# Weighted expert sums as 64x64 quarters in four banks, and conditioning products in four column groups

## The chip, the cores and the metric

The kernel runs on one core of a Trainium2 chip. The core has five engines that run side by side: TensorE (matrix products, with its own loading of weights), VectorE, ScalarE, GpSimd (in the profile POOL; here it issues the gathers) and SyncE (which issues plain transfers). The metric is the device time of one execution in microseconds (us). The kernel before took 2040.57 us, the median of three runs (2038.49 to 2043.5).

## The reference, cut to what matters

One layer of a decoder for 512 prompt rows and 8 sample rows of 1024 values, all in fp32. Two parts of it matter here. The first is the conditioning: `m = silu(c) @ w_ada + b_ada`, with nine rows of `c` (one prompt, eight samples) and 6144 columns, split into the six shifts, scales and gates. The second is the retrieval of experts, after the attention and the pooling:

```python
def block(args):                       # 128 rows at a time
    hb, eb, gb = args                  # rows, 8 heads x 16 experts each, their gates
    act = gelu(einsum('td,thkd->thk', hb, u_tab[eb]))
    return einsum('thk,thkd->td', gb * act, v_tab[eb])
```

So each of 512 rows has 128 experts of its own. For each one a row of 1024 values of `u_tab` is gathered for a dot product, and a row of `v_tab` to be added up, weighted by the gate times the activation. That is 2 x 512 x 128 rows of 4 KB, 537 MB, in four blocks of 128 rows.

## The kernel before, in words

Everything lives in one tensor, `arena`, of 128 partitions, and in eight banks of PSUM, each 128 partitions by 512 columns. The order of each engine is written out by hand; semaphores tie the engines together. A plan (`bank_plan`) lists what uses a bank in which order; each takes the next bank in turn, and TensorE waits until ScalarE ("A") or VectorE ("V") has read the bank's former content (`begin`, `wait_emptied`).

**Conditioning.** `w_ada` comes in twelve blocks of 512 columns (2 MB each) through a ring of three places that all weights of the first part share. SyncE issues a block when the use of the place's former content has ended. `ada_products(i)` (L1119 to L1123) is eight products that add up in one bank: the stationary side is a 128x9 piece of the transposed conditioning, the moving side 128x512 weights. ScalarE copies the 9x512 result out (L513), and `ada(i)` turns it with four transposes (L1130). VectorE adds the bias. Blocks 0 to 3 come first of all, since the first normalisation needs them; 4 to 6 stand behind the attention, 7 behind the branch products, 8 to 11 before the second normalisation.

**Experts.** A block of 128 rows has 32 steps of four expert slots each, in eight turns of four steps. A step goes through the engines so:
- GpSimd issues four gathers of 128 rows of `u_tab` and four of `v_tab` (L464), each into 128 partitions, one row to a partition. There are two sets of buffers for each table; a gather waits until the step before last has used its set.
- VectorE forms the four dot products (L956), and later the coefficients (L961).
- ScalarE applies the gelu (L614) and then writes four diagonal matrices, 128x128, with the coefficients on the diagonal (L618).
- TensorE multiplies each diagonal with the gathered 128x1024 rows in two halves of 512 columns, and adds up in two PSUM banks (L1351, `expert_step`). Blocks alternate between banks 0, 1 and 2, 3; `clear_sums` (L1342) zeroes them first.
- At a block's end VectorE multiplies the two banks by the gate `g2b` (L1001), adds the residual rows, which TensorE has transposed into two more banks (L1395), and SyncE stores the rows. This is `finish(b)`; it stands behind turn 0 of the next block.

In turn 0 VectorE's dot products read the normalised rows from SBUF; from turn 1 on they read them from PSUM, into which TensorE transposes them (L1402) after turn 0.

The first 16 steps of block 0 are interleaved with the products by the query weights (`pq`, L1104, 16 pieces of 0.5 MB) and the scores of the experts' keys (L1335, L1337), which route the tokens. Routing of the next block runs in VectorE's steps of the block before. In block 3 the eight sample rows are prepared between the turns, in banks 0 and 1, and their own gathers and sums come last (L1428, L1439).

## Time and profile before

| | us |
|---|---|
| median of three runs | 2040.57 |
| the profiled execution | 2038.34 |
| its span, first to last instruction | 2036.3 |
| TensorE busy in the span | 1662.0 |
| VectorE busy | 1075.1 |
| GpSimd busy | 1042.4 |
| ScalarE busy | 367.2 |
| expert products (L1351), busy | 1002.7 |

The span of a profiled execution is cut into stretches, and for each the profile gives the busy time of the engines, the granted share of TensorE's clock (1.00 is 2.4 GHz, 0.50 is 1.2 GHz) and what the transfers moved. The chain of waits follows the work that ended last back from the end: at each step it goes to what released the wait, so that a piece in it is on the path. A row of TensorE's timeline merges equal instructions; a bracket behind it tells how long the engine sat idle before and what ended that. An fp32 product appears as two records of weights and two of products.

### The profile page before, as it was taken

Reading aid. Unit: us, or ns where it says so; the run is one execution under the profiler, and the core shown is the slowest. Engines: PE = TensorE matmul, PEld = TensorE weight load, DVE = VectorE, ACT = ScalarE, POOL = GpSimd, SP = SyncE. Lnnn points to the kernel's source line nnn. Section 1 sums busy time; section 2 is a strip of 40 time slices with the busy share of each in tenths; the row PEclk is TensorE's granted clock in tenths of the full one; section 3 lists DMA queues with packets and bytes.
Section 4 is the critical chain, followed back from the end, with each engine's and each line's share of the span. In section 5 each row is a group of like instructions: output and inputs, shape, how many; then the busy total and the mean of one; then the engine's idle time right before and its main releaser. Section 6 shows DMA issues by size and latency. Waiting matters only on the chain.

```text
span 2036.3 us, 16401 instructions
## 1 busy us (share of the span) xinstructions
PE 1662.0 (82%) x4939; PEld 867.1 (43%) x4939; DVE 1075.1 (53%) x2685; ACT 367.2 (18%) x987; POOL 1042.4 (51%) x1066
## 2 busy tenths in 40 slices
PE   6899999999989995777767666767777776778878
PEld 2358874876756662333323222323333332333332
DVE  4111421314257676897566666647676664444443
ACT  2011343001212121112111111211112111111111
POOL 2100000000164555777757777757777775767774
PEclk9899899999989998989889999998899998889999
DMA  9423114144289877999989999989999998999996
GB/s 295 80 90 107 42 52 124 42 145 153 60 332 334 305 277 285 398 410 410 377 336 409 410 410 410 409 322 381 410 410 410 410 385 306 410 394 410 410 410 265
DMA packets 196406, 612.40 MB, mean 301 GB/s; under 512 B 21808, under 2 KB 39508, under 8 KB 196218
## 3 DMA queue, kind: packets, MB, share of 16 engines
q0 software_dynamic: 155216, 551.61, 70.1%
q1 hardware_dynamic: 41130, 60.04, 9.2%
q8 instruction: 32, 0.52, 0.1%
q14 instruction: 28, 0.23, 0.0%
HBM read 607.78 MB, written 3.59 MB: 300 GB/s over the span
## 4 chain that ended last, share of the span: by engine, by line
PE 50%; DMA 18%; POOL 16%; issue 7%; DVE 7%; ACT 1%; DVEq 1%; SPq 0%; ACTq 0%; POOLq 0%
PE psum L1351 22%; PE psum L1104 20%; DMA arena<-in_peer_v,arena 16%; POOL arena L464 16%; PE psum L1166 4%; DVE arena L956 3%; DMA arena<-in_w_in 1%; ACT arena L498 1%; DMA arena<-in_x_sample 1%; PE psum L1439 1%; PE psum L1193 1%; PE psum L1335 1%; DVE arena L868 0%; PE psum L1428 0%; DVE arena L869 0%
## 5 line engine op out<-in xcount | busy, mean ns | idle before, releaser
L1351 PE MATMUL psum<-arena 128*128 128x512 f32 x2048 | 1002.7, 647 | 324.8 <-DMA arena<-in_peer_v,arena 265.3
L1351 PEld LDWEIGHTS psum<-arena 128*128 128x128 f32 x2048 | 411.7, 206 | 901.8 <-issue 701.3
L464 POOL DMA_INDIRECT arena<-in_peer_u,arena x512 | 501.0, 978 | 399.1 <-issue 149.0
L956 DVE CUSTOM_DVE_ANT_0 arena<-arena,psum 128x1024 f32<-128x1024 f32 x400 | 464.6, 1218 | 327.8 <-DMA arena<-in_peer_u,arena 262.0
L464 POOL DMA_INDIRECT arena<-in_peer_v,arena x512 | 497.1, 971 | 179.5 <-issue 142.4
L1104 PE MATMUL psum<-arena 128*128 128x260 f32 (+2 forms) x1812 | 447.4, 407 | 10.6 <-ACT arena L498 8.0
L1104 PEld LDWEIGHTS psum<-arena 128*128 128x128 f32 (+1 forms) x1812 | 319.8, 180 | 128.4 <-issue 78.7
L618 ACT ACTIVATE arena<-arena 128x128 f32<-128x128 f32 x512 | 163.5, 390 | 271.6 <-DVE arena L961 271.6
L614 ACT ACTIVATE arena<-arena 128x4 f32<-128x4 f32 x128 | 26.2, 205 | 770.6 <-DVE arena L956 770.6
L498 ACT ACTIVATE arena<-psum 128x512 f32<-128x512 f32 (+9 forms) x181 | 75.6, 451 | 452.0 <-PE psum L1104 310.3
L956 DVE CUSTOM_DVE_ANT_0 arena<-arena 128x1024 f32<-128x1024 f32 x112 | 130.5, 1220 | 37.0 <-DMA arena<-in_peer_u,arena 36.7
L1166 PE MATMUL psum<-arena 128*128 128x512 f32 (+3 forms) x240 | 89.3, 533 | 8.0 <-DMA arena<-in_w_in 8.0
L456 POOL DMA_DIRECT2D arena<-in_peer_subkeys x1 | 1.2, 1197 | 160.1 <-DVE arena L828 160.1
L1166 PEld LDWEIGHTS psum<-arena 128*128 128x128 f32 (+1 forms) x240 | 41.2, 174 | 55.3 <-issue 43.8
L442 POOL DMA_DIRECT2D arena<-arena x2 | 1.0, 519 | 100.6 <-DVE arena L753 100.6
L961 DVE TENSOR_TENSOR arena<-arena 128x4 f32<-128x4 f32 x128 | 21.5, 168 | 54.4 <-ACT arena L614 34.9
L972 DVE COPY arena<-psum 128x512 f32<-128x512 f32 x16 | 11.0, 690 | 74.1 <-PE psum L1335 73.8
L956 DVE DVE_READ_ACCUMULATOR2_ANT arena<- 128x1 f32 x512 | 42.3, 83 | 0.0
L696 DVE TENSOR_TENSOR arena<-psum,arena 128x36 f32<-128x36 f32 x12 | 2.4, 196 | 75.5 <-PE psum L1130 75.5
L764 DVE SCALAR_TENSOR_TENSOR arena<-psum,arena 128x512 f32<-128x512 f32 (+1 forms) x16 | 9.2, 616 | 53.6 <-PE psum L1193 53.4
L744 DVE TENSOR_TENSOR arena<-arena 128x3200 f32<-128x3200 f32 x1 | 3.5, 3491 | 57.9 <-ACT arena L498 57.9
L868 DVE FIND_INDEX8 arena<-arena 128x8 uint32<-128x128 f32 (+3 forms) x99 | 32.6, 329 | 0.0
(200 smaller groups left out, 829.8 us busy)
## 6 DMA issues: line engine op xcount, KB each, us to landing
arena<-in_w_ada SPq DMA_DIRECT2D x12, 2048.0 KB, 8.5
arena<-in_w_in SPq DMA_DIRECT2D x6, 2048.0 KB, 19.1
arena<-in_peer_u,arena POOLq DMA_INDIRECT x520, 6.9
arena<-in_peer_v,arena POOLq DMA_INDIRECT x520, 7.0
arena<-in_peer_wq SPq DMA_DIRECT2D x16, 512.0 KB, 9.1
arena<-in_w_out SPq DMA_DIRECT2D x2, 2048.0 KB, 13.6
arena<-in_x_prompt SPq DMA_DIRECT2D x4, 512.0 KB
arena<-in_w_branch_attn SPq DMA_DIRECT2D x2, 1024.0 KB, 9.7
```

The lines of the kernel that those rows point to most:

```text
L464: pool.indirect_dma_start(out=buf[side * GS + i], out_offset=None, in_=table[0], in_offset=bass.IndirectOffsetOnAxis(ap=eidx[:, b, slot:sl ...
L498: ins = act.activation(out, in_, f, **kw)
L614: act.activation(gelus[:, side, :], acts[:, side, :], ACT.Gelu_apprx_tanh).then_inc(gelu_done, 1)
L618: ins = act.activation(diags[:, side * GS + i, :], ident, ACT.Copy, scale=coefs[:, side, i:i + 1])
L868: dve.max_index(i[:, 0:8], v[:, 0:8], s)
L956: ins = dve.tensor_tensor_reduce(rows_i, rows_i, h2n[:, b, :] if h is None else h, 1.0, 0.0, ALU.mult, ALU.add, acts[:, side, i:i + 1])
L961: dve.tensor_tensor(coefs[:, side, :], gelus[:, side, :], best[:, b, bass.ds(it * (TURN * GS) + k * GS, GS)], ALU.mult).then_inc(coef_read ...
L1104: ins = pe.matmul(out, a, b, start=(n == 0), stop=(n == len(pairs) - 1))
L1166: ins = pe.matmul(o, hT[:, k, cols(b)], wt[:, k, 0:n], start=(k == 0), stop=(k == C - 1))
L1193: ins = pe.matmul(o[:, i * 2 * P + lo:(i + 1) * 2 * P], qkT[r, j % 2 * 2 + i, cols(b)], qkT[r, 4, (b - 1) * P + lo:(b + 1) * P], start=Tru ...
L1335: ins = pe.matmul(o[:, b * P:(b + 1) * P], pq[:, m % 2, b * P:(b + 1) * P], skT[m], start=True, stop=True)
L1351: ins = pe.matmul(psum[:, 2 * (b % 2) + h, :], diags[:, side * GS + i, :], v_rows[side * GS + i][:, h * 512:(h + 1) * 512], start=False, s ...
```

## The change

Expert sums. A diagonal is now kept as 128x64: the upper 64 rows and the lower 64 rows each hold a 64x64 diagonal. ScalarE makes it by scaling `two_idents`, which is one identity above another. Each 128x128x512 product becomes two products of 64 rows by 64 columns. Slots are taken in pairs: the first of a pair adds its halves straight into banks 0 and 1, the second adds them crosswise (lower rows into the upper partitions and the reverse) into banks 2 and 3. All four banks now belong to one block; `clear_sums` clears four, and waits for the sum of the block before. `finish` swaps the halves of banks 2 and 3 back, adds them to banks 0 and 1, and then multiplies and adds as before. It now stands behind step 0 of the next block, not behind turn 0. TensorE's turns are written out instead of a loop.

Banks. From the second query product on, the plan has banks 4 to 7 instead of 2 to 7. The samples' pieces in block 3 use banks 6 and 7, every two steps, and the residual rows of block 3 are transposed last.

Conditioning. The stationary piece is padded from 9 to 32 columns, and the eight products go to four groups of 32 output partitions, two to each. ScalarE copies all 128 partitions, and `ada(i)` folds the groups with four products by `ada_fold`, a 128x9 matrix of ones where a group's row belongs, in place of the transposes.

```diff
-    bank_of = [i % BANKS if i < sums_from else 2 + (i - sums_from) % (BANKS - 2) for i in range(len(plan))]
+    bank_of = [i % BANKS if i < sums_from else 4 + (i - sums_from) % (BANKS - 4) for i in range(len(plan))]
...
-            copy(("ada_rows", i), ada_rows[i][0:9, :], bank(("ada_rows", i))[0:9, :])
+            copy(("ada_rows", i), ada_rows[i], bank(("ada_rows", i)))
...
-                ins = act.activation(diags[:, side * GS + i, :], ident, ACT.Copy, scale=coefs[:, side, i:i + 1])
+                ins = act.activation(diags[:, side * GS + i, :], two_idents, ACT.Copy, scale=coefs[:, side, i:i + 1])
...
+        dve.memset(scT[:, :, 9:ADA_M], 0.0)
+        dve.wait_ge(ident_loaded, 16)
+        dve.tensor_reduce(ada_fold, ident.rearrange("p (j r) -> p r j", r=ADA_M)[:, 0:9, :], X, ALU.add)
...
-            for i in range(2):
-                h = slice(i * 512, (i + 1) * 512)
-                ins = dve.tensor_tensor(y_rows[:, h], psum[:, 2 * (b % 2) + i, :], g2b[:, h], ALU.mult)
-            ins.then_inc(sum_read, 1)
+            both = y_rows.rearrange("p (a b) -> p a b", a=2)
+            dve.tensor_copy(both[0:HD], psum[HD:P, 2:4, :])
+            dve.tensor_copy(both[HD:P], psum[0:HD, 2:4, :])
+            dve.drain()
+            dve.tensor_tensor(both, both, psum[:, 0:2, :], ALU.add).then_inc(sum_read, 1)
             dve.wait_ge(sum_read, b + 1)
+            dve.tensor_tensor(y_rows, y_rows, g2b, ALU.mult)
+            dve.drain()
...
+            def first_turn(routing):
+                for k in range(TURN):
+                    step(b, 0, k, routing)
+                    if k == 0:
+                        finish(b - 1)
...
-            end(product(begin(("ada_rows", i))[0:9, :], [(scT[:, k, :], w[:, k, :]) for k in range(8)]))
+            o = begin(("ada_rows", i))
+            groups = P // ADA_M
+            for k in range(8):
+                j = k % groups
+                ins = pe.matmul(o[j * ADA_M:(j + 1) * ADA_M, :], scT[:, k, :], w[:, k, :], start=(k < groups), stop=(k >= 8 - groups))
+            end(ins)
...
-                ins = pe.transpose(o[:, n * 9:(n + 1) * 9], ada_rows[i][0:9, n * P:(n + 1) * P], ident[0:9, 0:9])
+                ins = pe.matmul(o[:, n * 9:(n + 1) * 9], ada_rows[i][:, n * P:(n + 1) * P], ada_fold, start=True, stop=True)
...
-            for i in range(GS):
+            lower, upper = slice(0, HD), slice(HD, P)
+            for pair in range(0, GS, 2):
                 for h in range(2):
-                    ins = pe.matmul(psum[:, 2 * (b % 2) + h, :], diags[:, side * GS + i, :],
-                                    v_rows[side * GS + i][:, h * 512:(h + 1) * 512],
-                                    start=False, stop=False, skip_group_check=True)
+                    hs = slice(h * 512, (h + 1) * 512)
+                    for i, bank_i, swapped in ((pair, h, False), (pair + 1, 2 + h, True)):
+                        for src in (lower, upper):
+                            dst = (upper if src is lower else lower) if swapped else src
+                            row = side * GS + i
+                            ins = pe.matmul(psum[dst, bank_i, :], diags[src, row, :], v_rows[row][src, hs],
+                                            start=False, stop=False, skip_group_check=True)
...
-            with pe.Fori(first, first + count) as it:
+            for it in range(first, first + count):
...
+        def residual_rows(b):
+            for i in range(2):
+                for c in range(4):
+                    ins = pe.transpose(psum[:, 4 + 2 * (b % 2) + i, c * P:(c + 1) * P], xT[:, 4 * i + c, cols(b)], ident)
+            ins.then_inc(x1_rows_ready, 1)
...
-            if b >= 2:
-                pe.wait_ge(sum_read, b - 1)
             if b:
-                clear_sums(b)
+                pe.wait_ge(sum_read, b)
+                clear_sums()
```

TensorE in the overlap of block 0 with the query products: query product (two halves of eight), scores of one key set, expert step. Before:

```order
L1104 MATMUL psum<-arena 128x260 x16
L1335 MATMUL psum<-arena 128x128 x4
L1337 MATMUL psum<-arena 8x128
L1351 MATMUL psum<-arena 128x512 x8
L1104 MATMUL psum<-arena 128x260 x16
```

and of the changed kernel (L1118, L1354, L1356 and L1376 are the same four in that order):

```order
L1118 MATMUL psum<-arena 128x260 x16
L1354 MATMUL psum<-arena 128x128 x4
L1356 MATMUL psum<-arena 8x128
L1376 MATMUL psum<-arena 64x512 x16
L1118 MATMUL psum<-arena 128x260 x16
```

The order stands; eight products of 128 rows have become sixteen of 64.

VectorE in turn 0 of block 1, around the place where the sum of block 0 is read. Before, it follows the coefficients (L961) of step 3, and the dot products (L956) after it already read PSUM:

```order
L917 CAST arena<-arena 128x16
L961 TENSOR_TENSOR arena<-arena 128x4
L1001 TENSOR_TENSOR arena<-psum,arena 128x512 x2
L1007 TENSOR_TENSOR arena<-arena,psum 128x512 x2
L945 UNCONDITIONAL_BRANCH
L945 ISA
L956 ISA arena<-arena,psum 128x1024
L956 ISA arena 128x1
```

and of the changed kernel, where it follows the coefficients (L968) of step 0, ahead of the dot products (L963) of step 1:

```order
L876 MATCH_REPLACE arena<-arena 128x128
L968 TENSOR_TENSOR arena<-arena 128x4
L1007 COPY arena<-psum 64x1024
L1008 COPY arena<-psum 64x1024
L1010 TENSOR_TENSOR arena<-arena,psum 128x1024
L1012 TENSOR_TENSOR arena<-arena 128x1024
L1017 TENSOR_TENSOR arena<-arena,psum 128x512 x2
L963 ISA arena<-arena 128x1024
L963 ISA arena 128x1
```

The sum has moved three steps forward, and two instructions on two halves have become six, of which the first three stand before the clear of the next block.

TensorE from the last steps of block 1 into block 2 of the changed kernel, the clear (L1361), the residual rows (L1411), turn 0, and the rows for the dot products (L1429):

```order
L1376 MATMUL psum<-arena 64x512 x448
L1361 MATMUL psum<-arena 128x512 x4
L1411 MATMUL psum<-arena 128x128 x8
L1376 MATMUL psum<-arena 64x512 x64
L1429 MATMUL psum<-arena 128x128 x8
L1376 MATMUL psum<-arena 64x512 x448
```

The same sequence stood there before, with L1342 (two products) for the clear and loops for the turns; the wait ahead of the clear was for the block before last, and is now for the last.

## Rows read from the trace of the kernel before

**Rows 1.** Stretches: length, busy (count) of PE, PEld, DVE, ACT, POOL, clock, DMA share, GB/s
```profile
594.00:747.00 153.00, 153.00 (x583) 101.89 (x582) 100.37 (x292) 33.58 (x89) 77.84 (x80) 1.00 0.84 296
1150.00:1200.00 50.00, 35.32 (x80) 14.49 (x78) 33.29 (x88) 8.49 (x25) 37.41 (x40) 1.00 1.03 410
1450.00:1500.00 50.00, 39.10 (x77) 16.18 (x78) 33.27 (x89) 8.70 (x26) 36.84 (x40) 0.90 1.03 410
```

**Rows 2.** Groups by line and shape, TensorE: records | busy us, mean ns | idle before
```profile
L1351 PE MATMUL psum<-arena 128*128 128x512 f32 x2048 | 1002.7, 647 | 324.8 <-DMA arena<-in_peer_v,arena 265.3 <-ACT arena L618 59.5
```

**Rows 3.** Chain of waits, overlap of block 0: start, length, what (records)
```profile
594.34 7.06 PE psum L1351 x16
601.41 7.01 PE psum L1104 x32
...
609.63 7.06 PE psum L1351 x16
```

**Rows 4.** Chain of waits, two pieces of the steady stretch
```profile
1140.34 9.22 DMA arena<-in_peer_v,arena
...
1149.68 7.14 PE psum L1351 x16
...
1485.28 7.41 DMA arena<-in_peer_v,arena
...
1492.81 8.84 PE psum L1351 x16
```

**Rows 5.** Timeline of TensorE, the scores of block 3: three windows of growing length
```profile
299.58 0.91 PE L1193 MATMUL psum<-arena 64*128 64x256 f32 x3
...
299.58 1.13 PE L1193 MATMUL psum<-arena 64*128 64x256 f32 x4
...
299.58 2.96 PE L1193 MATMUL psum<-arena 64*128 64x256 f32 x16
```

**Rows 6.** Timeline of TensorE, conditioning block 1; chain of waits, first query weights
```profile
34.04 7.04 PE L1104 MATMUL psum<-arena 128*9 128x512 f32 x16
...
41.11 23.72 DMA arena<-in_w_in
```

**Rows 7.** Timelines of TensorE and SyncE, 320 to 430 us
```profile
326.24 1.06 PE L1280 MATMUL psum<-arena 128*128 128x8 f32 x8
...
341.82 0.41 PE L1130 MATMUL psum<-arena 9*128 9x9 f32 x4
...
428.72 57.78 PE L1104 MATMUL psum<-arena 128*128 128x260 f32 x256 [2.58 <-issue]
...
418.06 0.99 SPq L399 DMA_DIRECT2D arena<-in_w_out  x2
```

**Rows 8.** Timelines of TensorE and VectorE, transfers issued, 485 to 520 us
```profile
489.96 13.90 PE L1104 MATMUL psum<-arena 128*9 128x512 f32 x32
...
519.92 4.59 PE L1328 MATMUL psum<-arena 128*128 128x128 f32 x40
...
495.33 4.97 DVE L704 TENSOR_TENSOR arena<-arena 128x520 f32<-128x520 f32 x8
...
505.94 3.73 DVE L716 TENSOR_SCALAR arena<-arena 128x512 f32<-128x512 f32 x8
...
arena<-in_w_ada SPq DMA_DIRECT2D x2, 2048.0 KB, 7.9
```

**Rows 9.** Timelines of TensorE, VectorE and GpSimd, block 0 to block 1
```profile
1015.83 8.55 PE L1351 MATMUL psum<-arena 128*128 128x512 f32 x16 [5.00 <-DMA arena<-in_peer_v,arena]
...
1006.82 1.28 DVE L1001 TENSOR_TENSOR arena<-psum,arena 128x512 f32<-128x512 f32 x2
1025.51 1.22 DVE L956 CUSTOM_DVE_ANT_0 arena<-arena,psum 128x1024 f32<-128x1024 f32 x1 [16.09 <-PE psum L1402]
...
1030.44 0.95 POOL L464 DMA_INDIRECT arena<-in_peer_u,arena  x1 [11.34 <-DVE arena L956]
```

**Rows 10.** Timeline of GpSimd, the last value gathers of block 3
```profile
1992.45 0.94 POOL L464 DMA_INDIRECT arena<-in_peer_v,arena  x1 [5.86 <-PE psum L1351]
```

More of the change, by code:

```diff
@@ L55 @@
 TURN = 4
+ADA_M = 32
 K_ID = 0
@@ L232, in decoder_layer @@
     vecT = at(take(68), 68)
-    ones = at(take(P), P)
-    scT = at(take(C * 9), C * 9, C)
+    ones = at(take(1), 1)
+    scT = at(take(C * ADA_M), C * ADA_M, C)
+    ada_fold = at(take(9), 9)
     gqk = at(take(2 * HD), 2 * HD, 2)
@@ L288, in decoder_layer @@
     o_diag = take(2 * GS * P)
-    diags = at(o_diag, 2 * GS * P, 2 * GS)
+    diags = at(o_diag, 2 * GS * HD, 2 * GS)
     pq = at(take(2 * TT), 2 * TT, 2)
@@ L307, in decoder_layer @@
     zeros = at(take(P), P)
+    two_idents = at(take(HD), HD)
     o_y = take(D)
@@ L507, in _ @@
         wait_filled(act, ("vecT",))
-        copy(("cT",), scT, bank(("cT",))[:, 0:72].rearrange("p (a b) -> p a b", a=C))
+        copy(("cT",), scT[:, :, 0:9], bank(("cT",))[:, 0:72].rearrange("p (a b) -> p a b", a=C))
         for c in range(C):
@@ L855, in _ @@
         scv = sc.rearrange("p (b m) n -> p b m n", b=5)
-        link(dve.memset(zeros, 0.0))
+        dve.memset(zeros, 0.0)
+        link(dve.tensor_tensor(two_idents, ident[:, 0:HD], ident[:, HD:P], ALU.add))
         dve.memset(gelus, 0.0).then_inc(u_used, AHEAD)
@@ L1021, in _ @@
                     steps[1] = 0
-                    turn(0)
+                    first_turn(lambda head, part: route_head(b + 1, head, part))
                     steps[1] = None
-                    finish(b - 1)
                 else:
@@ L1042, in _ @@
                 dve.wait_ge(sample_rows_loaded, 16 * PH)
-                one_turn(0, lambda head, part: route(HS, hs_in[0:HS], hs_best[0:HS], hs_expert[0:HS], part))
-                finish(b - 1)
+                first_turn(lambda head, part: route(HS, hs_in[0:HS], hs_best[0:HS], hs_expert[0:HS], part))
                 v = hs_best[0:HS].unsqueeze(1)
@@ L1110, in mean_squares @@
                 pe.wait_ge(square_sum_ready, n)
-                ins = pe.matmul(o, ones, squares[:, 0, half(h)], start=True, stop=True)
+                ins = pe.matmul(o, ones.broadcast_to((P, P)), squares[:, 0, half(h)], start=True, stop=True)
                 end(ins)
@@ L1151, in _ @@
         wait_emptied(pe, ("cT",))
+        pe.wait_ge(ones_ready, 1)
         ada_products(0)
-        pe.wait_ge(ones_ready, 1)
         mean_squares(1)
@@ L1337, in subkey_scores, with clear_sums @@
             end(pe.matmul(begin(("scs", m))[0:S, 0:NK], pq[:, m % 2, T:TT], skT[m], start=True, stop=True))
-        def clear_sums(b):
-            for i in range(2):
-                pe.matmul(psum[:, 2 * (b % 2) + i, :], zeros, zeros[:, 0:1].broadcast_to((P, 512)),
+        def clear_sums():
+            for i in range(4):
+                pe.matmul(psum[:, i, :], zeros, zeros[:, 0:1].broadcast_to((P, 512)),
                           start=True, stop=False, skip_group_check=True)
@@ L1369, in _ @@
             if m == OVER_FROM:
-                for i in range(2):
+                for i in range(4):
                     wait_emptied(pe, plan[max(j for j in range(len(plan)) if bank_of[j] == i)][0])
-                clear_sums(0)
+                clear_sums()
             if 0 <= m - 1 - OVER_FROM < OVER * TURN:
@@ L1392, in _ @@
                 pe.wait_ge(u_used, AHEAD + b * STEPS)
-            for i in range(2):
-                for c in range(4):
-                    ins = pe.transpose(psum[:, 4 + 2 * (b % 2) + i, c * P:(c + 1) * P], xT[:, 4 * i + c, cols(b)], ident)
-            ins.then_inc(x1_rows_ready, 1)
+            if b < NB - 1:
+                residual_rows(b)
             if b:
@@ L1409, in _ @@
                 pe.wait_ge(sample_spread, 2)
-                pe.wait_ge(sum_read, b)
                 for i in range(2):
-                    ins = pe.matmul(psum[:, 0, i * S:(i + 1) * S], hs_spread[0:PH * S, i, :], kc[0:PH * S, K_SEQ:K_END], start=True, stop=True)
+                    ins = pe.matmul(psum[:, 6, i * S:(i + 1) * S], hs_spread[0:PH * S, i, :], kc[0:PH * S, K_SEQ:K_END], start=True, stop=True)
                 ins.then_inc(sample_turned, 1)
@@ L1420, in _ @@
                     for c in range(C):
-                        ins = pe.transpose(psum[0:S, c // 4, c % 4 * P:(c % 4 + 1) * P], src[:, c, first:first + S], ident)
+                        ins = pe.transpose(psum[0:S, 6 + c // 4, c % 4 * P:(c % 4 + 1) * P], src[:, c, first:first + S], ident)
                     ins.then_inc(sample_x_ready, 1)
```

26 lines of the change are left out of this document (14 added, 12 removed).

## The prediction

> **What bounds the kernel now.** The profiled execution took 2038.3 us (span 2036.3 us), 2.2 us under the 2040.6 us median of the three runs. I read the stretches first, then the chain of waits inside each, then single engines where the chain changes hands. There are three regimes.
>
> From 0 to about 525 us the chain runs mostly through TensorE, except where a weight load lands last [rows 6 to 8]. From 594 to 747 us products of the query weights alternate with expert steps of block 0: TensorE is busy for all 153.00 us, while the transfers run at 296 GB/s [rows 1]. The chain there holds TensorE pieces alone: 7.06 us for an expert step, 7.01 us for a query product, and 15.29 us from one step to the next (609.63 - 594.34) [rows 3].
>
> From about 800 us on the transfers are the limit: 410 GB/s with TensorE busy 35.32 of 50 us [rows 1]. The reader should see why a shorter TensorE step gives nothing there. The chain runs TensorE, gather issue, transfer, TensorE. Around 1140 us a step took 7.14 us and its transfer 9.22 us; around 1485 us a step took 8.84 us and its transfer 7.41 us [rows 4]. What the step lost, the transfer gave back: the two add up to 16.36 and 16.25 us. A step moves eight gathers of 0.524 MB, 4.19 MB, and at 410 GB/s that is 10.23 us. TensorE's 7 to 9 us fit under it. The changes from block to block are different: there the gathers stop for 11.34 us [rows 9].
>
> **What a quarter product costs.** An expert step is now 8 products, and the trace has 2048 records for 1024 of them [rows 2], so each fp32 product runs as two, 7.06/16 = 0.44 us apart, about 0.43 with the tail of the last one taken off. The change makes 16 products of 64 rows by 64 columns. Streaming 512 columns takes as long on a quarter as on the whole array, so all depends on how many quarters stream together. Four together: 16 x 2 x 0.43 / 4 = 3.4 us. Two: 6.9 us. None: 13.8 us.
>
> The trace has one place with half-array products, the scores: eight records on the lower 64 rows, then eight on the upper. Their spacing is 1.13 - 0.91 = 0.22 us, so 16 in a row would take 1.13 + 12 x 0.22 = 3.77 us; they took 2.96 us [rows 5]. Some 0.8 us, three to four records, ran beside others. Had products started strictly one after the other, only one spacing of 0.22 us could have gone, so products on the upper rows overtook lower ones that still waited. That is what four quarters need, since the second record of a quarter must wait for the first while the next quarter's starts. I take 3.4 us. No row shows two column groups on the same rows; that is the open half.
>
> The Trainium skill speaks against this twice. "TensorE: Matmul & The Clock Gate", Part 3, says that packed matmuls start and end strictly in program order. By that rule every second record holds up the next quarter, a step takes 16 x 0.43 = 6.9 us, and the sum keeps only the conditioning terms. The scores above do not agree with it. "TensorEngine Tiling (Array Packing)", Gotcha 1, says that different row tiles cannot use one PSUM bank at once. Here bank h takes lower rows into its lower half and upper rows into its upper half; by that rule quarters run in pairs, with the same 6.9 us. No run here shows two row groups in one bank.
>
> **The sum, part by part.**
>
> Conditioning products: eight products of nine columns take 7.04 us [rows 6]. In four column groups they take 1.9 us if all four stream together, 8 x 0.43 + 0.43 = 3.9 us if only the second record of one and the first of the next overlap, 7.04 if none. I take 3.6 us, near the middle bound, since no row shows more. Each fold becomes four full products of nine columns. Its nearest row is eight records of 128x8 in 1.06 us against 0.41 us for the transposes it replaces: 0.65 us more [rows 7].
> - Blocks 0 to 3: the query weights are issued at 41.11 us, when block 1 is done, and land 23.72 us later; TensorE waits for them [rows 6]. Block 1 ends 3.4 us sooner, so does the wait. Gain 3.4 (bounds 0 and 5.1).
> - Blocks 4 to 6: on TensorE's own path, 3 x (3.4 - 0.65) = 8.3 (bounds -2 and 13.5).
> - Block 7: nothing. The output weights are issued at 418.06 us, when a ring slot is free, and the next product starts at 428.72 us after a wait [rows 7]. What block 7 saves, that wait takes.
> - Blocks 8 to 11: from 489.96 us, two products now end at 496.9, the folds at 499.0, block 10 at 502.6, block 11 (its weights are issued when block 8 is done at 493.6 and land 7.9 us later) at 506.0, the folds at 508.1, against 519.92 [rows 8]. VectorE's own chain would not be late: its normalisation ends at 495.33 + 4.97 = 500.3, after block 9 now, and its last pieces are the row of 3.73 us and a few short ones, so about 505. Gain 11.8 (bounds -2.6 and 14.9).
>
> Overlap: TensorE needs 7.01 + 1.2 + 3.4 = 11.6 us a step with the score products, plus some tenths for switching between whole array and quarters. Late next are the transfers: a step's 4.19 MB and 0.52 MB of query weights, 4.72 MB at 410 GB/s, 11.5 us. VectorE's busy time is 100.37 us in ten steps, 10.0 us each [rows 1]. With three engines within 1.6 us I take 12.3 us, a gain of 3.0 on each of the 11 steps from the first expert step to the last query product: 33 (bounds 0 and 38). That the query products have four banks instead of six costs nothing: they are read out by ScalarE before the next expert step can start. If that cover fails, one step slips by at most the 3.4 us of that expert step. The clear of four banks instead of two, once, lies in the wait for the first gathers.
>
> Block changes: VectorE cannot start turn 1 until TensorE has ended the fourth step of turn 0 and the transposes: 16.09 us of idle, with the gathers waiting behind it [rows 9]. The step there took 8.55 us. TensorE will idle longer between steps. The granted clock is 1.00 (2.4 GHz) in 1150 to 1200 us, where steps take 7.14, and 0.90 in 1450 to 1500 [rows 1, 4], where steps that begin at the lower level (1.2 GHz) take 8.84, 1.7 more. So I price a quarter step here at 3.4 + 1.7 = 5.1 us, at worst 6.9 (all at half clock). Gain 3.5 to 1.7 at each of four places: 11.
>
> The added wait: TensorE's first step of a block stands behind the new sum, which stands behind VectorE's step 0. Nothing but the clear and the residual transposes is queued in between. VectorE's sum is two copies of 1024 columns, one addition, one product and the residual: five passes of about 1.28 us, as the pair of 512 columns shows [rows 9], 6.3 us instead of 2.6. It moves from the end of turn 0, where VectorE idled, to its start, where the next dot products are due, and the gathers behind them. TensorE's last step of the old block now ends 2 to 4 us sooner, which pays for 3.7. I take 0 (bounds 0 and 3.7 at each of three).
>
> Steady steps: 0; the transfer hides them. Scaling the 64-column diagonals is shorter on ScalarE, hidden likewise. The straight-line instruction stream instead of a loop: bounded by 0 and the 5 us by which a quarter step stays under 10.23; I take 0.
>
> Tail: the last value gather waited 5.86 us for TensorE [rows 10]; about 3.5 come back, and the longer sum takes 3.7. I take 0.
>
> Sum: 3.4 + 8.3 + 11.8 + 33 + 11 = 67.5. Against the profiled execution 2038.3 - 67.5 = 1970.8 us, on the scale of the median 1973 us.
>
> **The rivals.**
> - Quarters run only in pairs (program order, or one bank per row group): step 6.9, no overlap gain and nothing at block changes, conditioning 23.5 gained, 3.7 lost in the tail: 2040.6 - 23.5 + 3.7 = 2021 us. Against it: the scores' overtaking.
> - Two column groups on the same rows do not stream together. Then a step is 8 x 2 x 0.43 = 6.9 us, conditioning stays at 7.04, and what was added shows: seven folds on the path, 4.6 us, and the longer sum at three changes and the tail, up to 14.8, less 2 for the overlap. 2045 to 2058, taken as 2050 us: slower. It decides as soon as a step costs about what it did. For it: no row has two column groups at work. Against it: the array did take two row groups at once.
> - Quarters stream one by one: 13.8 us exceeds 10.23, so some 112 steps lose 3.5 us and 11 lose 6.7: about 2500 us. The scores speak against it.
>
> **How the numbers follow.** Forecast 66%, own range 1950 to 1995 us (its bounds: conditioning all four together, or overlap gains of half). Pairs 12%, columns 17%, one by one 5%. To hold 8 in 10 the range goes from 1950 over the pairs' case to 2032. About 6 us (0.3%) is what a measurement tells from no change. Faster: 66 + 12 = 78%; of the columns' 17, 4 fall within 0.3% and 13 beyond; slower 13 + 5 = 18%.
>
> **What would show it.** Expert steps of 3.4 to 4 us in the overlap, and 12 to 12.5 us between them; about 5 us later on, with the transfer in the chain longer by what the step lost and still 410 GB/s; conditioning products of 2 to 4 us; the wait before 428.72 grown instead of the time shortened. Steps near 7 us there, or conditioning at 7 us, make the forecast wrong; steps over 10 us turn its sign.

## The result, and the profile after

The changed kernel takes 1959.15 us, the median of four runs (1951.51 to 1962.64), against 2039.53 us for the kernel before on the same chip. The ratio is 0.960, with a 95% interval from 0.956 to 0.963: 4% faster. The forecast was 1973 us, in a range from 1950 to 2032. The profiled execution took 1961.6 us, 76.8 us under the profiled one of before.

The sum had 67.5 us. To see which of its terms hold, follow one event after another through TensorE's timelines of both traces and note how much earlier it comes (us):

| event | before | after | earlier by | this term | predicted |
|---|---|---|---|---|---|
| first query, key and value product | 64.87 | 49.06 | 15.8 | 15.8 | 3.4 |
| first branch product | 361.68 | 333.96 | 27.7 | 11.9 | 8.3 |
| first product by `w_out` | 428.72 | 403.10 | 25.6 | -2.1 | 0 |
| first product by the experts' query weights | 524.34 | 490.42 | 33.9 | 8.3 | 11.8 |
| first expert step | 576.24 | 543.18 | 33.1 | -0.9 | 0 |
| rows of block 0 for the dot products | 805.0 | 742.5 | 62.5 | 29.4 | 33 |
| end of block 3's last expert step | 2009.65 | 1927.89 | 81.8 | 19.3 | 11 |
| end of the span | 2036.3 | 1959.6 | 76.7 | -5.1 | 0 |

The rows of these events that stand nowhere else, of the kernel before and then of the changed one (start, length, what, count; the last step of block 3 ends 7.13 us behind 2002.52):

```profile
361.68 63.31 PE L1104 MATMUL psum<-arena 128*128 128x260 f32 x272 [0.77 <-ACT arena L498]
...
524.34 14.19 PE L1104 MATMUL psum<-arena 128*128 128x260 f32 x64
...
576.24 9.88 PE L1351 MATMUL psum<-arena 128*128 128x512 f32 x16 [9.53 <-DMA arena<-in_peer_v,arena]
...
805.05 1.04 PE L1402 MATMUL psum<-arena 128*128 128x128 f32 x8
...
2002.52 7.13 PE L1351 MATMUL psum<-arena 128*128 128x512 f32 x16 [1.88 <-DMA arena<-in_peer_v,arena]
```

```profile
490.42 7.18 PE L1118 MATMUL psum<-arena 128*128 128x260 f32 x32
...
543.18 5.46 PE L1376 MATMUL psum<-arena 64*64 64x512 f32 x32 [7.86 <-DMA arena<-in_peer_v,arena]
...
742.54 1.04 PE L1429 MATMUL psum<-arena 128*128 128x128 f32 x8
```

**Quarter products.** The first view is the grouping by line and shape, the second the timeline of TensorE in the overlap with the query products (start, length, what, count).

```profile
L1376 PE MATMUL psum<-arena 64*64 64x512 f32 x4096 | 685.8, 827 | 555.8 <-DMA arena<-in_peer_v,arena 516.2 <-ACT arena L621 39.6
```

```profile
594.63 0.66 PE L1376 MATMUL psum<-arena 64*64 64x512 f32 x4
...
594.63 1.09 PE L1376 MATMUL psum<-arena 64*64 64x512 f32 x8
...
594.63 3.67 PE L1376 MATMUL psum<-arena 64*64 64x512 f32 x32
```

The three rows are one step, seen in windows of growing length. Within the first 0.07 us four records have started; the next four start between 0.42 and 0.57 us, and all 32 of the step are done in 3.67 us, where 16 records took 7.06 [rows 3]. Twice the records in half the time: four quarters stream at once. The group has twice the records of [rows 2] and 685.8 us in place of 1002.7.

**The overlap and the steady stretch.** Stretches, with the columns of [rows 1]:

```profile
560.00:740.00 180.00, 148.59 (x896) 91.40 (x889) 137.09 (x404) 36.40 (x111) 120.88 (x112) 0.91 0.96 354
1100.00:1150.00 50.00, 24.93 (x160) 7.14 (x160) 33.54 (x90) 7.64 (x26) 37.63 (x40) 0.83 1.03 409
1420.00:1470.00 50.00, 33.08 (x160) 8.85 (x160) 33.19 (x91) 7.64 (x26) 37.13 (x40) 0.66 1.03 409
```

The first stretch takes in the overlap, which ends at 688 us, and 52 us behind it. There the transfers now run at 354 GB/s (360 from 543 to 688 us alone), where they had 296, and TensorE is no longer busy all the time. In the steady stretch nothing came back: 409 GB/s, where there were 410. The chain of waits there (start, length, what) shows why:

```profile
1133.63 11.22 DMA arena<-in_peer_v,arena
...
1144.89 5.04 PE psum L1376 x32
...
1432.16 9.78 DMA arena<-in_peer_v,arena
...
1441.98 6.67 PE psum L1376 x32
```

Step and transfer add up to 16.26 and 16.45 us, against 16.36 and 16.25 before [rows 4]. The second step is slower by 1.63 us at a granted clock of 0.66, and its transfer shorter by 1.44. The granted clock of the whole span fell from 0.94 to 0.83, while TensorE idled more, and in this stretch that cost nothing.

**Conditioning.** The timeline of TensorE, first two blocks, first fold, and the first product by the query, key and value weights (the bracket is the idle time before, and what ended it):

```profile
26.10 1.92 PE L1141 MATMUL psum<-arena 128*32 128x512 f32 x16
...
35.06 3.49 PE L1141 MATMUL psum<-arena 128*32 128x512 f32 x16
...
38.48 1.06 PE L1149 MATMUL psum<-arena 128*128 128x9 f32 x8
...
49.06 88.43 PE L1185 MATMUL psum<-arena 128*128 128x512 f32 x240 [2.82 <-DMA arena<-in_w_in]
```

Eight products that took 7.04 us [rows 6] take 1.92: all four column groups stream together, on the same 128 rows. Behind a pause of TensorE they take 3.49. The stretches of just these two blocks (columns of [rows 1]) show why: a granted clock of 1.00 and of 0.54, so nearly all of the second ran at 1.2 GHz.

```profile
26.10:28.02 1.92, 1.92 (x18) 0.42 (x16) 1.82 (x4) 0.34 (x2) 0.00 (x0) 1.00 1.04 383
35.06:38.55 3.49, 3.49 (x18) 0.67 (x17) 2.67 (x2) 0.64 (x1) 2.77 (x1) 0.54 1.05 387
```

The fold's four products cost the 1.06 us that [rows 7] gave. The first query weights land 10.39 us after their issue, not 23.72 [rows 6], as the chain of waits has it:

```profile
38.62 10.39 DMA arena<-in_w_in
```

**Later events of the first part,** the same timeline. The wait before `w_out` grew from the 2.58 us in [rows 7] to 7.41, as predicted; block 11 and the 40 transposes behind its folds now come behind a pause of TensorE and take 3.64 and 7.23 us (4.59 in [rows 8]).

```profile
333.96 11.35 PE L1118 MATMUL psum<-arena 128*128 128x260 f32 x43 [2.37 <-DMA arena<-in_w_branch_pool]
...
403.10 22.07 PE L1118 MATMUL psum<-arena 128*128 128x260 f32 x91 [7.41 <-issue]
...
476.35 3.64 PE L1141 MATMUL psum<-arena 128*32 128x512 f32 x16 [4.17 <-DMA arena<-in_w_ada]
...
483.35 7.23 PE L1347 MATMUL psum<-arena 128*128 128x128 f32 x40
```

**Change from block 0 to block 1.** TensorE's clear for block 1 and its last step of turn 0 of block 1; then GpSimd's two stops:

```profile
917.53 5.40 PE L1361 MATMUL psum<-arena 128*128 128x512 f32 x8 [3.88 <-DVE arena L1010]
...
952.69 5.51 PE L1376 MATMUL psum<-arena 64*64 64x512 f32 x32 [5.41 <-DMA arena<-in_peer_v,arena]
```

```profile
924.95 0.94 POOL L467 DMA_INDIRECT arena<-in_peer_u,arena  x1 [2.90 <-DVE arena L963]
...
964.41 0.95 POOL L467 DMA_INDIRECT arena<-in_peer_u,arena  x1 [6.96 <-DVE arena L963]
```

The stop of the gathers at the end of turn 0 shrank from 11.34 us [rows 9] to 6.96, and a new one of 2.90 us stands at its start, where the longer sum is. It is the same at the other changes: the stops where VectorE waits for the rows in PSUM were 13.98, 11.34, 11.97 and 11.78 us in blocks 0 to 3 and are 11.73, 6.96, 6.96 and 7.85, and the new ones are 2.90, 4.15 and 5.40 in blocks 1 to 3.

**Tail.** Last step of block 3 and the sample rows' sums, from the chain of waits:

```profile
1922.58 5.31 PE psum L1376 x32
1927.92 1.23 DVE arena L1007
...
1934.21 4.96 DVE arena L1086 x9
...
1940.16 14.42 PE psum L1466 x30
```

From the end of the last step to the end of the span it is now 31.7 us (before 26.7). The sum's passes stand ahead of the samples' dot products (L1086), and the sample products start 12.3 us behind the last step, not 8.6. They also take longer, 15.27 us at a granted clock of 0.91 against 13.89 at 1.00.

### The profile page after: what moved, and what is told of

Read it like the earlier page. It is cut to its first block, busy times and chain, and to the rows that moved or that the text cites. A ratio compares the mean times of both kernels' runs of the same rounds, so it can differ in the third digit from the quotient of the medians.

```text
span 1959.6 us, 20512 instructions
## 1 busy us (share of the span) xinstructions
PE 1324.5 (68%) x7051; PEld 656.3 (33%) x7051; DVE 1089.3 (56%) x2696; ACT 338.7 (17%) x986; POOL 1043.7 (53%) x1066
## 4 chain that ended last, share of the span: by engine, by line
PE 34%; POOL 25%; DMA 17%; DVE 12%; issue 10%; DVEq 1%; ACT 1%; SPq 0%; ACTq 0%; POOLq 0%
POOL arena L467 25%; PE psum L1118 15%; DMA arena<-in_peer_v,arena 15%; PE psum L1376 10%; DVE arena L963 6%; PE psum L1185 5%; ACT arena L501 1%; PE psum L1141 1%; PE psum L1466 1%; DMA arena<-in_x_sample 1%; PE psum L1212 1%; DMA arena<-in_w_in 1%; DVE arena L875 1%; DMA arena<-in_w_ada 0%; DMA arena<-in_w_branch_pool 0%
## 5 line engine op out<-in xcount | busy, mean ns | idle before, releaser
L1376 PE MATMUL psum<-arena 64*64 64x512 f32 x4096 | 685.8, 827 | 555.8 <-DMA arena<-in_peer_v,arena 516.2
L467 POOL DMA_INDIRECT arena<-in_peer_u,arena x512 | 495.6, 968 | 354.0 <-issue 149.0
L963 DVE CUSTOM_DVE_ANT_0 arena<-arena,psum 128x1024 f32<-128x1024 f32 x400 | 464.7, 1219 | 325.4 <-DMA arena<-in_peer_u,arena 265.1
L467 POOL DMA_INDIRECT arena<-in_peer_v,arena x512 | 503.7, 984 | 170.1 <-issue 144.9
L1376 PEld LDWEIGHTS psum<-arena 64*64 64x64 f32 x4096 | 195.2, 186 | 1029.7 <-DMA arena<-in_peer_v,arena 619.8
L1118 PE MATMUL psum<-arena 128*128 128x260 f32 (+2 forms) x1620 | 367.9, 387 | 17.6 <-ACT arena L501 7.8
L1118 PEld LDWEIGHTS psum<-arena 128*128 128x128 f32 (+1 forms) x1620 | 302.3, 191 | 82.2 <-issue 30.0
L621 ACT ACTIVATE arena<-arena 128x64 f32<-128x64 f32 x512 | 136.3, 337 | 269.7 <-DVE arena L968 267.6
L501 ACT ACTIVATE arena<-psum 128x512 f32<-128x512 f32 (+8 forms) x181 | 76.8, 450 | 368.3 <-PE psum L1118 140.3
L963 DVE CUSTOM_DVE_ANT_0 arena<-arena 128x1024 f32<-128x1024 f32 x112 | 130.5, 1221 | 10.1 <-DMA arena<-in_peer_u,arena 9.8
L1185 PEld LDWEIGHTS psum<-arena 128*128 128x128 f32 (+1 forms) x240 | 40.7, 172 | 49.8 <-issue 42.9
L968 DVE TENSOR_TENSOR arena<-arena 128x4 f32<-128x4 f32 x128 | 21.7, 170 | 51.9 <-ACT arena L617 32.5
L963 DVE DVE_READ_ACCUMULATOR2_ANT arena<- 128x1 f32 x512 | 42.3, 83 | 0.0
## 6 DMA issues: line engine op xcount, KB each, us to landing
arena<-in_w_ada SPq DMA_DIRECT2D x12, 2048.0 KB, 11.3
arena<-in_w_branch_attn SPq DMA_DIRECT2D x2, 1024.0 KB, 10.4
```

The costliest lines, as they stand in the source:

```text
L467: pool.indirect_dma_start(out=buf[side * GS + i], out_offset=None, in_=table[0], in_offset=bass.IndirectOffsetOnAxis(ap=eidx[:, b, slot:sl ...
L501: ins = act.activation(out, in_, f, **kw)
L621: ins = act.activation(diags[:, side * GS + i, :], two_idents, ACT.Copy, scale=coefs[:, side, i:i + 1])
L963: ins = dve.tensor_tensor_reduce(rows_i, rows_i, h2n[:, b, :] if h is None else h, 1.0, 0.0, ALU.mult, ALU.add, acts[:, side, i:i + 1])
L968: dve.tensor_tensor(coefs[:, side, :], gelus[:, side, :], best[:, b, bass.ds(it * (TURN * GS) + k * GS, GS)], ALU.mult).then_inc(coef_read ...
L1118: ins = pe.matmul(out, a, b, start=(n == 0), stop=(n == len(pairs) - 1))
```

## The experiments

The theory from the traces: the conditioning's gain reaches the end undiminished, because the stretch behind it was bound by TensorE; the experts' gain lies in the overlap and at the changes of block, where the gathers stop for VectorE. Each run is compared with runs of the kernel before on its own chip (medians 2039.7 to 2042.5 us).

**1 and 2. Each half alone.** cond_only takes the conditioning lines of the diff and leaves the expert sums; experts_only does the reverse. The core of each:

```diff
+                ins = pe.matmul(o[j * ADA_M:(j + 1) * ADA_M, :], scT[:, k, :], w[:, k, :], start=(k < groups), stop=(k >= 8 - groups))
```

```diff
+                            ins = pe.matmul(psum[dst, bank_i, :], diags[src, row, :], v_rows[row][src, hs],
```

> The kernel before with the conditioning half of the change alone (column groups, fold), experts as they were. Theory A: what the conditioning gained ahead of the experts (33.1 us at the first expert step, 576.24 to 543.18) carries to the end, since the stretch behind it is bound by TensorE as before: first expert step near 543 us, time 2040 - 33 = 2007 us (2002 to 2012). Rival B: part of the earlier start comes from the rest of the change, or the experts give it back: over 2018 us.

> The changed kernel with the old conditioning. Theory A: the two halves of the change add up; the experts' half is 76.8 - 33.1 = 44 us, so 1996 us (1990 to 2002), with the first expert step near 576 us and steps of 3.7 us in the overlap. Rival B: the halves need each other (the sum of both gains is off from 77 us by over 10).

Measured: 2002.24 us (ratio 0.981, 0.978 to 0.984) and 1995.88 us (0.979, 0.977 to 0.981). That is 37.5 and 43.9 us, 81.4 in sum, against 80.4 for the whole change: the halves add up. The rows are the first expert step of cond_only and of experts_only, from TensorE's timelines.

```profile
540.61 9.46 PE L1361 MATMUL psum<-arena 128*128 128x512 f32 x16 [9.53 <-DMA arena<-in_peer_v,arena]
```

```profile
577.83 6.29 PE L1366 MATMUL psum<-arena 64*64 64x512 f32 x32 [7.55 <-DMA arena<-in_peer_v,arena]
```

The 36 us of earlier start are the conditioning's alone (576.24 before), and they reach the end.

**3. Why the first weights landed sooner.** The kernel before with one wait changed:

```diff
-        wait_filled(pool, ("ss", 1, 1))
+        wait_filled(pool, ("q", 0))
         for cache, tile in ((cache_k, ktile), (cache_v, vtile)):
```

> The kernel before, with GpSimd's loads of the two caches held back until the first query product has ended; nothing else changed. Theory A: in the kernel before, the first query weights were slow to land (23.72 us after 41.11) because the caches' small packets ran beside them, and in the changed kernel, issued 2.5 us sooner, they got ahead of these packets (10.4 us). Then here they land 10 to 12 us after issue and the products start at 51 to 54 us instead of 64.87; what of it stays at the end is 4 to 12 us, 2028 to 2036 us. Rival B: the landing time has another cause (how the transfers were queued): it stays near 23 us and the time at 2040 us. Rival C: the weights land early, but the packets hit the next weights as hard, and nothing is left by 362 us.

Measured: 2033.79 us (0.996, 0.995 to 0.998): 6 us. The first row is the kernel before, the second this one (TensorE's timelines), the third the landing of the weights in this one (transfers issued from 40 to 60 us: size, median us to landing).

```profile
64.87 89.32 PE L1166 MATMUL psum<-arena 128*128 128x512 f32 x240 [8.03 <-DMA arena<-in_w_in]
```

```profile
58.71 88.55 PE L1166 MATMUL psum<-arena 128*128 128x512 f32 x240 [1.63 <-DVE arena L716]
```

```profile
arena<-in_w_in SPq DMA_DIRECT2D x2, 2048.0 KB, 7.8
```

Without the caches' packets beside them 2 MB land in 7.8 us (median of two), not 23.72, and TensorE waits for VectorE instead. So theory A holds, with the start later than its 51 to 54 us: VectorE is late next. Of the 15.8 us at the first products, 6.2 are this wait, and the other 9.6 (58.71 - 49.06) are left for the shorter chain of blocks 1 to 3: TensorE's folds end at 46.23 us in the changed kernel, its transposes at 57.08 here. What the weights met is seen in the packets, first of the kernel before from 50 to 56 us, then of the changed kernel from 38 to 44 us: 810 packets of the queue that holds the caches' loads, at 148 GB/s in all, and none of that queue in the changed kernel.

```profile
DMA packets 1441, 0.89 MB, mean 148 GB/s; under 512 B 810, under 2 KB 1257, under 8 KB 1441
...
q0 software_dynamic: 810, 0.09, 39.9%
```

```profile
DMA packets 993, 2.02 MB, mean 336 GB/s; under 512 B 16, under 2 KB 16, under 8 KB 992
...
q1 hardware_dynamic: 992, 2.00, 95.5%
```

The earlier issue is only half of the head start. The first packet of that queue came at 43.34 us before, 2.2 us behind the issue of the weights; in the changed kernel it comes at 46.06 us, 7.4 us behind it. Of these 5.2 us more, 2.5 are the earlier issue, and 2.7 come from packets that start later. GpSimd issues the first cache load 1.0 us later (35.78 us, was 34.76), behind a product that takes TensorE 2.07 us after a pause of 5.03, where it took 1.11; where the rest comes from was not tried.

**4 and 5. The order of the quarters.** The same sixteen products; in order_grouped four of a quarter in a row, in order_pairs two.

```diff
+            for swapped in (False, True):
+                for src in (lower, upper):
+                    for i in range(int(swapped), GS, 2):
+                        for h in range(2):
```

```diff
+            for pair in range(0, GS, 2):
+                for i, swapped in ((pair, False), (pair + 1, True)):
+                    for src in (lower, upper):
+                        for h in range(2):
```

> The changed kernel with the same sixteen products of a step in another order: all four of one quarter, then all four of the next, where before neighbours in the order always went to different quarters. Theory A: products are taken in order with little looking ahead, so a quarter runs alone except at the three borders: 16 x 2 x 0.43 = 13.8 us a step less up to 0.9 at each border, 11 to 13.8 us; that exceeds the 10.23 us of a step's transfers, about 2 to 3 us on each of 112 steps and 6 to 8 on 11, 2250 to 2400 us. Rival B: each quarter has work of its own waiting far ahead and they run side by side in any order: 3.7 us a step, 1960 us.

> As order_grouped, but only two products (four records) of a quarter stand together before the next quarter's two. Theory A, read from order_grouped's trace (the second quarter's first record starts together with the first quarter's fifth): up to four records of a quarter can wait while products behind them go to another quarter. Four records in a row then hold nobody up: steps of 3.7 to 4.5 us in the overlap and 1955 to 1970 us. Rival B: a quarter's work starts when half of the former quarter's is done, whatever its length: starts 0.86 us apart, eight groups, 16 x 0.43 = 6.9 us or more a step and about 2020 us.

Measured, one run each: 2122.46 and 1950.37 us. Neither theory gave order_grouped's 8.98 us a step. Its timeline, again in growing windows, and then a whole step:

```profile
578.38 0.64 PE L1376 MATMUL psum<-arena 64*64 64x512 f32 x1
...
578.38 1.93 PE L1376 MATMUL psum<-arena 64*64 64x512 f32 x4
...
578.38 2.42 PE L1376 MATMUL psum<-arena 64*64 64x512 f32 x6
...
578.38 8.98 PE L1376 MATMUL psum<-arena 64*64 64x512 f32 x32
```

The first four records come one after the other; then two start within 0.07 us (windows to 580.10 and 580.17 us): the fifth of the first quarter and the first of the second. (The trace doesn't name quarters; this is read from the order of the products.) So a quarter with eight records lets the next one begin when four of its own are left. Three such delays of 1.78 us and eight records of 0.43 make 8.8 us, which is the step but for 0.2. That rule gave the expectation for order_pairs, and its steps take what the change's own order takes:

```profile
587.35 3.74 PE L1376 MATMUL psum<-arena 64*64 64x512 f32 x32
```

**6. The rows for the dot products earlier.** The changed kernel, in blocks 1 to 3:

```diff
-                expert_turns(b, 0, 1)
+                for k in range(2):
+                    expert_step(b, 0, k)
                 pe.wait_ge(y_ready, b)
...
             ins.then_inc(h_psum_ready, 1)
+            if b:
+                for k in range(2, TURN):
+                    expert_step(b, 0, k)
```

> The changed kernel with the rows that the dot products of turns 1 to 7 read transposed after step 1 of turn 0, not after step 3 (blocks 1 to 3). Theory A: VectorE's wait at the end of turn 0 (59.3 us in four waits) stops the gathers for 6.96 us, and from 955 to 975 us the transfers moved 283 and 271 GB/s instead of 410, 6.5 us of transfer time lost; this wait goes at three places: 10 to 19 us less, 1940 to 1949 us. Rival B: VectorE is held by something else there (the diagonals, TensorE's steps) and the stop only moves: within 4 us of 1959.

Measured: 1937.91 us (0.950, 0.948 to 0.952), 21 us less than the changed kernel. The stretch around the change to block 1, in the changed kernel and here:

```profile
890.00:1000.00 110.00, 57.16 (x336) 18.23 (x328) 74.81 (x180) 17.93 (x54) 77.59 (x77) 0.79 0.97 375
```

```profile
890.00:1000.00 110.00, 63.49 (x360) 19.50 (x352) 79.30 (x196) 18.15 (x55) 81.31 (x82) 0.78 1.02 401
```

That is more than theory A's 10 to 19 us. 26 GB/s more over 110 us is 2.9 MB, 7 us of transfer at 409 GB/s. It is so at all three changes: TensorE's clears for blocks 1, 2 and 3 and its first piece for the samples come 1.6, 6.9, 14.4 and 22.1 us earlier than in the changed kernel, 5 to 8 us more from each to the next, which is all of the gain. The stops that went had 6.96, 6.96 and 7.85 us. What the change left of this stop was worth more than the 19 us that it took at the changes of block.

**7. The second half of the sum later.** The changed kernel with `finish` cut in two:

```diff
             dve.tensor_tensor(both, both, psum[:, 0:2, :], ALU.add).then_inc(sum_read, 1)
+        def finish_rest(b):
             dve.wait_ge(sum_read, b + 1)
...
+                    if k == 1:
+                        finish_rest(b - 1)
```

> The changed kernel with the second half of the block's sum (the gate product and the residual, 2.5 us of VectorE) behind step 1 of the next block instead of ahead of its dot products. Theory A: the longer sum at the start of turn 0 costs what it holds up the gathers (a stop of 2.90 us at 924.95), so some 2.5 us at each of three places come back: 1952 us, and the added wait of the prediction cost 6 to 9 us. Rival B: transfers already queued cover it (from 915 to 925 us they moved 411 GB/s): 1957 to 1961 us, and the added wait cost nothing.

Measured: 1951.95 us (0.956, 0.954 to 0.958). The interval touches that of the changed kernel (0.956 to 0.963), so the 7 us between the medians are not settled. The trace speaks for some 5: the stops of 2.90, 4.15 and 5.40 us are gone, and the four events of run 6 come 2.5, 3.0, 5.3 and 7.2 us earlier. The first of them stands ahead of what was edited and shows the scatter between two executions; the three changes gave 0.5, 2.3 and 1.8 us. The first is the stretch of run 6: 378 GB/s here, against 375.

```profile
890.00:1000.00 110.00, 57.01 (x336) 18.21 (x332) 77.44 (x193) 17.93 (x55) 79.35 (x78) 0.77 0.97 378
```

**8. The last sum behind the samples' dot products.**

```diff
-        finish(NB - 1)
         def sample_coefs(q):
...
         sample_coefs(1)
+        finish(NB - 1)
```

> The changed kernel with the last block's sum behind the sample rows' dot products and coefficients instead of ahead of them. Theory A: the tail from the last expert step to the end grew from 26.7 to 31.8 us because the longer sum (6.3 us) stands ahead of the samples' chain; behind it, it lies beside TensorE's 15 us of sample products: 5 to 6 us less, 1953 to 1955 us. Rival B: the samples' own gathers land no sooner, so nothing: 1959 us.

Measured: 1953.60 us (0.958, 0.956 to 0.961), not told apart from the changed kernel by time. Its timeline:

```profile
1913.42 3.67 PE L1375 MATMUL psum<-arena 64*64 64x512 f32 x32 [0.28 <-DMA arena<-in_peer_v,arena]
...
1925.92 16.66 PE L1465 MATMUL psum<-arena 128*8 128x512 f32 x32 [7.80 <-DVE arena L1076]
```

and from its chain of waits, the last of the samples' gathers:

```profile
1916.90 7.60 DMA arena<-in_peer_u,arena
```

From the end of the last step (1917.09) to the end of the span (1946.8) it is 29.7 us, 2.0 less than in the changed kernel, not 5 to 6. The sample products start 8.8 us behind the last step, not 12.3: the samples' gathers land late next, as rival B had it. And the products take 16.66 us at a granted clock of 0.83, where they took 15.27 at 0.91.

**9 and 10. Together.** combined has the edits of 6 to 8. combined_b0 adds that of 3, and in block 0:

```diff
-                        one_turn(it, two_parts, h_psum(0))
-                    dve.wait_ge(h_psum_ready, 1)
-                    loop(OVER, TURNS - 1, turn_of_two)
+                        one_turn(it, two_parts, None if it is OVER else h_psum(0))
+                    steps[1] = OVER
+                    turn_of_two(OVER)
+                    steps[1] = None
+                    dve.wait_ge(h_psum_ready, 1)
+                    loop(OVER + 1, TURNS - 1, turn_of_two)
```

> The changed kernel with the edits of early_rows, sum_split and tail_order together. Theory A: each takes away its own stop of the gathers or of the tail, so they add up: 1959.2 - 21.2 - 7.2 - 2 to 5.6 = 1925 to 1929 us, under both kernels. Rival B: with the stop at the end of turn 0 gone, queued transfers cover the one at its start, so the split sum is worth nothing more: 1932 to 1937 us.

> As combined, and two edits more: in block 0 the first turn after the query products reads the normalised rows from SBUF, as turn 0 of the other blocks does, so that VectorE doesn't wait for their transposes; and the cache loads wait for the first query product, as in before_cache_later. Theory A: the gathers' stop of 12.07 us at 746.82 us goes, which a change of block without it (6.5 us of transfer time for a stop of 6.96) puts at 8 to 11 us, and TensorE's wait of 2.82 us for the first query weights goes: 9 to 14 us under combined. Rival B: at that place the diagonals and TensorE are late as well, so that the stop only moves: 0 to 4 us under combined.

Measured: 1926.78 us (0.944, 0.942 to 0.946) and 1923.51 us (0.942, 0.940 to 0.945), both under the two kernels of this document. combined is where the sum of the single runs was, and under rival B's 1932 to 1937 us. Its interval doesn't touch that of run 6, so the split sum and the moved tail are worth something together (11 us by the medians), which runs 7 and 8 left open. The second step is 3.3 us by the medians, not 9 to 14 but in rival B's 0 to 4, and the two are not told apart. A stretch of combined, then of combined_b0:

```profile
710.00:760.00 50.00, 24.48 (x152) 9.39 (x144) 32.23 (x103) 5.21 (x18) 29.87 (x30) 0.74 0.81 291
```

```profile
710.00:760.00 50.00, 27.89 (x172) 10.18 (x164) 40.27 (x126) 7.24 (x26) 39.84 (x34) 0.72 0.95 338
```

So the stop did go, and 5.7 us of transfer came back (47 GB/s over 50 us); 1.5 of it was lost again right behind (395 GB/s against 410 from 760 to 800 us). The cache loads' edit was worth little here: the first query product starts at 48.19 us instead of 49.68, where in combined it waits for VectorE and no longer for the weights.

## Why the prediction was right, and where its terms were off

The time fell inside the forecast's own range, by the mechanism that it named: quarters and column groups that stream together, a gain in the conditioning, the overlap and the changes of block, and none in the steady stretch. That the sum came within 9.2 us of the 76.7 in the trace is in part luck, since larger errors of both signs cancel. Term by term:

- **Quarters at 3.4 us: right.** 3.67 us, four at once. What the prediction read from the scores [rows 5], that products overtake others that still wait, is the reason, and runs 4 and 5 show how far it goes: runs of four records of a quarter cost next to nothing, runs of eight let the next quarter in at the fifth. The scores fit this: four records alone, four beside others, four alone are 1.13 + 8 x 0.22 = 2.9 us, where 2.96 were measured. In order_grouped the second quarter's first record started beside the first quarter's fifth. By the Trainium skill, "TensorE: Matmul & The Clock Gate", Part 3, matmuls start in program order, so it would not have started before the eighth; the trace disagrees. Lower and upper rows wrote their halves of one bank together, at 3.67 us a step. By the Trainium skill, "TensorEngine Tiling (Array Packing)", Gotcha 1, different row tiles cannot use one bank at once, which would give pairs and 6.9 us; the trace disagrees here too.
- **Conditioning at 3.6 us: too dear.** It is 1.92, the lower bound, and 3.5 to 3.6 only where TensorE comes from a pause. For blocks 4 to 6 the difference is the missing gain: 11.9 instead of 8.3. It would be 13.4 if the wait before the branch products had not grown from 0.77 to 2.37 us. For blocks 8 to 11 the bound was near, but TensorE now waits 4.17 us for weights and runs at a granted clock of 0.50 to 0.62 behind that: 8.3 instead of 11.8. (The prediction's sum for these blocks takes a product at 3.4 to 3.6 us by turns; with 3.6 throughout it ends at 508.6 us, a gain of 11.3.)
- **Blocks 0 to 3 at 3.4 us: the worst miss, 12.4 us.** The step said: the query weights are issued when block 1 is done and land 23.72 us later, so they land 3.4 us sooner. It took a landing time for fixed that was itself a collision. The 23.72 us held the caches' small packets, and run 3 shows that these made it so long: 7.8 us without them. With the weights 2.5 us sooner and the packets 2.7 us later, most of the weights got through ahead. With all but 2.82 us of that wait gone, the shorter chain counts.
- **Block 7 at 0: 2.1 us lost.** The mechanism was right: the wait for `w_out` grew from 2.58 to 7.41 us and took what was saved. Most of the rest is the branch products ahead of it, 57.9 us at a granted clock of 0.97 against 56.3 at 1.00.
- **Overlap at 33 us: 29.4.** Twelve steps from 543.18 to 684.30 are 12.83 us apart, not 12.3. TensorE's own period is 12.0, and value gathers land up to 1.6 us late in about every second step: the transfers are late next, as forecast. The four banks of the query products cost nothing, as forecast: in the overlap none of these products waits.
- **Block changes at 11 us: 19.3 with the rest of blocks 1 to 3.** At the change to block 1 the step was 5.51 us (priced 5.1, with the lower clock as expected), 3.0 under the 8.55 of before. The stop shrank by 4.4: the transfer ahead of that step was shorter too, 6.1 instead of 7.6 us in the two chains. That is 1.5 us more there; why it was shorter was not tried. The four stops shrank by 2.3, 4.4, 5.0 and 3.9 us, 15.6 in all; the other 3.7 of the row, and what the new stops took, are not traced to a place.
- **The added wait at 0: some 0.5 to 2.5 us a block.** The new stops at the start of turn 0 are this wait. Run 7's time allows 7 us in all, its trace about 5, and neither is settled by itself.
- **Steady steps at 0: right.** The straight-line instruction stream was not tried alone; the rows of the chain there show no wait for it.
- **Tail at 0: 5.1 us lost.** The prediction set 3.5 us of faster step against 3.7 of longer sum. The step came ahead of the point from which the tail is counted, so the table has its gain in the row above. The longer sum did cost its 3.7 (12.3 us to the first sample product instead of 8.6), and the sample products 1.4 more, at the lower granted clock. Run 8 took 3.4 of the first away, lost 1.4 to a still lower clock, and returned 2.0.

The errors are +12.4, +3.6 and +8.3 against -2.1, -3.5, -0.9, -3.6 and -5.1: 24.3 us one way and 15.2 the other; with rounding, 9.2 are left.

## What to carry to other kernels

A landing time from a trace is no constant: before you subtract from an issue time, see what else the queues carried while it landed, since a start a little sooner, or a crowd of small packets a little later, can change it by more than half. When an engine stops being the bound, follow its last wait at each change of stage: here the stop that the change only shortened was worth 21 us more, for moving eight transposes two steps ahead. If you pack products into quarters of the array, let neighbours in the order go to different quarters, or keep each run short.

## What the runs showed of the hardware

- Four 64x64 quarters stream at once, with two row groups in one bank's two halves: 32 records in 3.67 us, and four column groups on the same rows: 16 records in 1.92 us.
- How far products pass waiting ones is limited: runs of four records per quarter cost nothing (3.74 us a step), runs of eight cost 8.98 us.
- Two megabytes of weights landed in 7.8 us or in 23.7, without or with the small packets of a 508 KB load beside them; with a head start of 7.4 us on these packets it was 10.4.
